# V's projection jobs first, K's three rounds behind; V's weights loaded as f32 in four pieces and cast on the chip

## The chip, the cores and the metric

The kernel runs on the 8 cores of one Trainium2 chip. Each core computes one batch element of 2048 tokens by itself; no core waits for another. The time of a run is device microseconds of the slowest core.

## The reference, cut to what matters

One decoder layer. From one normalised input come the projections q, k, v, u and two gates; attention and a pooling branch are merged by the gates, and an MLP follows. The part that matters here is the first line and what becomes of k and v:

```python
h = rms_norm(x, norm_mix[l])
proj = h @ w_in[l]                                  # [B,S,IN_WIDTH]
q, k, v, u, g_a, g_p = jnp.split(proj, splits, axis=-1)
q = partial_rope(rms_norm(q.reshape(B, S, ATTN_HEADS, HEAD_DIM), q_norm[l]), pos)
k = partial_rope(rms_norm(k.reshape(B, S, ATTN_HEADS, HEAD_DIM), k_norm[l]), pos)
v = v.reshape(B, S, ATTN_HEADS, HEAD_DIM)
o_attn = moba_attention(q, k, v)                    # 256-token blocks, own block plus 3 chosen by q . mean(k)
o_pool = multiscale_pool(u, w_pool_grp[l], pool_scale[l])
merged = sigmoid(g_a) * (o_attn @ w_up_attn[l]) + sigmoid(g_p) * (o_pool @ w_up_pool[l])
x = x + merged @ w_out[l]
x = x + jnp.square(jax.nn.relu(rms_norm(x, norm_mlp[l]) @ w_ff1[l])) @ w_ff2[l]
```

x is f32, 2048 x 1024 a core; each of the weights of q, k, v and u is 1024 x 512 in f32, 2.1 MB.

## The kernel before, in words

The tokens are cut into 16 tiles of 128. A tile of x is loaded into one of four slots (`p0_load`, L382, on SP's queue), squared and summed on ScalarE (`p0_sq`, L388), multiplied by its reciprocal root and the gain on VectorE (`p0_mul`, L399), transposed on TensorE (`p0_tr`, L406, eight transposes) and copied to `hT` by VectorE or ScalarE (`p0_ev`, through `evict`, L372 and L377). Then come four jobs for each tile, one each for K, V, U and Q: eight matmuls of 128 x 512 into one of four PSUM banks (`proj_mm`, L429). A weight lies in `wqkvu[cg]` as bf16, loaded in two halves by GpSimd's queue (`load_w`, L338), which casts on the way; a job waits for the first half before its first four matmuls and for the second before the others.

A V job is only evacuated (`v_ev`). A K or Q job goes on: square on ScalarE (`qk_sq`, L435), reduction on VectorE (`qk_red`, L440), root on ScalarE (`qk_root`, L444), scaling on VectorE (`qk_scale`, L451 to L457), which frees the bank, rope on VectorE or GpSimd (`qk_rope`, L468 to L476), transposes on TensorE (`qk_tr`, L483; for K with sums over the tile, L489) and evacuation. A U job is evacuated and goes through band matmuls (L516, L520). When all of K is there, `make_kT2` copies kT in two halves (SP), and behind each half loads `c_ind` twice on GpSimd's queue, which waits for the copy. Attention's matmuls (L880) need both.

The order of all this is not written out. A planner at the start of the program takes tasks with a priority (the place of their job in the list `jobs`), an estimated duration and an earliest time, lays them on the engines in a list schedule, and the program is emitted in the order of the planned starts. On the chip each engine works through its own instructions in that order and waits in place for what is not ready; SP and GpSimd do the same with the loads that they issue. In `jobs` round r holds K of tile r, V of tile r-3, U of tile r-12 and Q of tile r-7:

```python
for cg, lag in ((CG_K, 0), (CG_V, 3), (CG_U, U_LAG), (CG_Q, 7)):
```

The first loads are written by hand in `first_loads`; later weights are tasks (`wq`, `wu`) that wait until a given x slot is written. When the planned attention begins, U jobs that are left are mixed into its steps. Behind this come gates, output projection and MLP.

## Time and profile before

| | before |
|---|---|
| three runs | 954.8, 955.9, 956.35 us, median 955.9 |
| the profiled run | 953.49 us, its span 952.4 us on core 7 (cores 947.3 to 952.4) |
| TensorE busy | 913.4 us, 96% of the span |
| VectorE, ScalarE, GpSimd busy | 461.5, 381.0, 75.3 us |
| 0 to 40 us | TensorE busy 18.6 us, DMA share 0.91 |
| 40 to 140 us | TensorE busy 92.6 of 100 us, VectorE 80.8 |

A row of a timeline names a start and a length in us, the engine, the line of the program, output and input, and how many instructions of the kind stand behind one another; in brackets stands how long the engine was idle before it and what ended that. Nearly all tiles are views of one buffer, so most names read `raw`, and lines tell the steps apart. "PE" is TensorE, "DVE" VectorE, "ACT" ScalarE, "POOL" GpSimd.

### The profile page before, as it was taken

The numbers are of one execution on the slowest core, as the hardware profiler recorded it, in microseconds if no ns is written. First come the engines' busy times: TensorE is split into PE (matmuls) and PEld (weight loads), VectorE is DVE, ScalarE is ACT, GpSimd is POOL, SyncE is SP. The second block draws the span as 40 slices with busy tenths as digits, with TensorE's granted clock in tenths as the row PEclk, the third lists the DMA queues.
The fourth block names the chain that finished last, engine by engine and source line by source line (L and its number), as shares of the span: only waits on it lengthen the run. The fifth ranks groups of instructions, "written<-read, shape, count | busy, mean of one in ns | idle before, by whom it ended". The sixth has DMA issues, their size and how long they took to land.

```text
span 952.4 us, 17253 instructions; the slowest of 8 cores (947.3 to 952.4 us)
## 1 busy us (share of the span) xinstructions
PE 913.4 (96%) x5772; PEld 469.2 (49%) x5772; DVE 461.5 (48%) x876; ACT 381.0 (40%) x738; POOL 75.3 (8%) x133
## 2 busy tenths in 40 slices
PE   3798999899999999999999999999999999999997
PEld 1344555667767764444444444444444444444443
DVE  2578877555532333434775444434444444444443
ACT  2566666798899982222004344031111221111120
POOL 4212110321000000100001000000000000000000
PEclk9899999999999999999999999999999999999999
DMA  8942023523433337793989904250064100001113
GB/s 196 212 121 68 2 73 89 85 44 76 65 65 63 68 59 130 155 216 79 194 131 154 140 1 57 36 86 1 1 89 59 31 1 1 1 0 77 60 64 155
DMA packets 57895, 76.31 MB, mean 80 GB/s; under 512 B 27792, under 2 KB 46224, under 8 KB 57552
## 3 DMA queue, kind: packets, MB, share of 16 engines
q0 software_dynamic: 24288, 40.28, 27.5%
q1 hardware_dynamic: 33520, 34.92, 13.5%
q8 instruction: 49, 0.80, 0.3%
q14 instruction: 38, 0.31, 0.1%
HBM read 98.41 MB, written 8.39 MB: 112 GB/s over the span
## 4 chain that ended last, share of the span: by engine, by line
PE 87%; DMA 6%; DVE 3%; issue 2%; ACT 1%; SPq 0%; POOL 0%; DVEq 0%; ACTq 0%; POOLq 0%
PE bank L1339 23%; PE bank L1313 23%; PE bank L986 10%; PE bank L429 8%; PE bank L880 6%; PE bank L1223 6%; PE bank L918 3%; PE bank L1000 3%; PE bank L1005 3%; DMA raw<-w_qkvu 3%; DMA raw<-x 2%; DMA raw<-w_slice 1%; PE bank L483 1%; DVE raw L399 0%; DVE raw L457 0%
## 5 line engine op out<-in xcount | busy, mean ns | idle before, releaser
L1320 ACT ACTIVATE raw<-bank 128x512 f32<-128x512 f32 x128 | 76.4, 597 | 375.8 <-PE bank L1313 317.2
L1313 PE MATMUL bank<-raw 128*128 128x512 bf16 x1024 | 223.1, 379 | 0.0
L1339 PE MATMUL bank<-raw 128*128 128x512 bf16 x1024 | 223.1, 379 | 0.0
L887 ACT ACTIVATE raw<-bank 128x512 bf16<-128x512 f32 x288 | 152.6, 613 | 19.3 <-PE bank L918 17.6
L1313 PEld LDWEIGHTS bank<-raw 128*128 128x128 bf16 x1024 | 100.4, 98 | 120.7
L1339 PEld LDWEIGHTS bank<-raw 128*128 128x128 bf16 x1024 | 100.0, 98 | 121.0
L1322 DVE SCALAR_TENSOR_TENSOR raw<-bank,raw 128x512 bf16<-128x512 f32 x128 | 88.5, 692 | 140.8 <-ACT raw L1320 140.7
L1345 DVE SCALAR_TENSOR_TENSOR raw<-bank,raw 128x512 f32<-128x512 f32 x128 | 96.1, 751 | 112.7 <-PE bank L1339 112.4
L429 PE MATMUL bank<-raw 128*128 128x512 bf16 x512 | 125.9, 395 | 13.5 <-DMA raw<-w_qkvu 7.6
L986 PE MATMUL bank<-raw 128*128 128x512 bf16 x512 | 122.5, 379 | 0.4 <-DMA raw<-w_slice 0.3
L880 PE MATMUL bank<-raw 128*128 128x256 bf16 x576 | 101.7, 272 | 1.8 <-ACT raw L887 1.2
L918 PEld LDWEIGHTS bank<-raw 128*128 128x128 bf16 x1088 | 70.9, 98 | 26.3 <-issue 1.1
L429 PEld LDWEIGHTS bank<-raw 128*128 128x128 bf16 x512 | 48.8, 100 | 70.0 <-issue 24.8
L918 PE MATMUL bank<-raw 128*128 128x65 bf16 x1088 | 79.8, 193 | 0.8 <-DVE raw L927 0.7
L1011 DVE SCALAR_TENSOR_TENSOR raw<-raw,bank 128x512 f32<-128x512 f32 x64 | 43.8, 686 | 73.5 <-PE bank L1005 56.0
L986 PEld LDWEIGHTS bank<-raw 128*128 128x128 bf16 x512 | 49.4, 98 | 49.6 <-issue 2.4
L991 ACT ACTIVATE raw<-bank 128x512 f32<-128x512 f32 x64 | 38.3, 598 | 73.3 <-PE bank L986 69.7
L1223 PE MATMUL bank<-raw 128*128 128x512 bf16 x256 | 55.4, 379 | 0.0
L1223 PEld LDWEIGHTS bank<-raw 128*128 128x128 bf16 x256 | 25.0, 98 | 30.2
L880 PEld LDWEIGHTS bank<-raw 128*128 128x128 bf16 x576 | 37.1, 97 | 4.8 <-issue 2.5
L140 POOL DMA_DIRECT2D raw<-w_ff x16 | 14.0, 880 | 283.6 <-PE bank L1313 86.1
L372 ACT ACTIVATE raw<-bank 128x512 bf16<-128x512 f32 (+1 forms) x39 | 25.9, 670 | 18.6 <-PE bank L429 14.7
(91 smaller groups left out, 604.1 us busy)
## 6 DMA issues: line engine op xcount, KB each, us to landing
raw<-x SPq DMA_DIRECT2D x32, 512.0 KB, 6.3
raw<-w_ff POOLq DMA_DIRECT2D x16, 1024.0 KB, 12.4
...
out<-raw SPq DMA_DIRECT2D x16, 512.0 KB, 2.6
raw<-w_qkvu POOLq DMA_DIRECT2D x8, 512.0 KB, 12.9
...
raw<-w_out POOLq DMA_DIRECT2D x4, 512.0 KB, 13.6
raw<-c_ind POOLq DMA_DIRECT2D x4, 256.0 KB, 6.2
```

What stands on the lines that cost most here:

```text
L429: t.group("pe", [lambda e, c=c: e.matmul(bank_f(bk), lhsT=hT[:, c, tt * 128:(tt + 1) * 128], rhs=wqkvu[cg][:, c, :], start=(c == 0), stop= ...
L880: fns.append(lambda e, kt=kt, j=j: e.matmul(bank_f(sb_)[:, j * 256:(j + 1) * 256], lhsT=ksel[:, pr, kt * 128:(kt + 1) * 128], rhs=qTz[:, h ...
L887: t.op("act", lambda e: e.activation(out=pt, in_=bank_f(sb_), func=AF.Exp, scale=0.125), reads=hb[sb_], writes=[b_PT[si % NPT]])
L918: fns.append(lambda e, dst=dst, c0_=c0_, kt=kt, ql=ql, last=last: e.matmul(dst, lhsT=pt[:, c0_:c0_ + 128], rhs=v_aug[:, kt, h, :], start=( ...
L986: t.group("pe", [lambda e, c=c: e.matmul(bank_f(bk), lhsT=w[:, c, :], rhs=hT[:, c, T0:T0 + 512], start=(c == 0), stop=(c == 7)) for c in c ...
L1011: t.op("dve", lambda e: e.scalar_tensor_tensor(out=dst, in0=dst, scalar=1.0, in1=bank_f(bk), op0=ALU.add, op1=ALU.mult), reads=hb[bk] + [b ...
L1223: t.group("pe", [lambda e, c=c, bk=bk, hf=hf: e.matmul(bank_f(bk), lhsT=mT[tt // 4][:, c, (tt % 4) * 128:(tt % 4 + 1) * 128], rhs=wout[:, ...
L1313: t.group("pe", [lambda e, c=c, j=j, bk=bk: e.matmul(bank_f(bk), lhsT=ffw1[s][:, c, j * 128:(j + 1) * 128], rhs=hT[:, c, tg * 512:(tg + 1) ...
L1320: t.op("act", lambda e, bk=bk, si_=si_: e.activation(out=sqz[si_], in_=bank_f(bk), func=AF.Square), reads=hb[bk], writes=[b_sqz[si_]])
L1322: t.op("dve", lambda e, bk=bk, si_=si_, j=j: e.scalar_tensor_tensor(out=a1T[ab][:, j, :], in0=bank_f(bk), scalar=0.0, in1=sqz[si_], op0=AL ...
L1339: t.group("pe", [lambda e, j=j, bk=bk, hf=hf, i=i: e.matmul(bank_f(bk), lhsT=a1T[ab][:, j, i * 128:(i + 1) * 128], rhs=ffw2[s][:, j, hf * ...
L1345: t.op("dve", lambda e, bk=bk, dst=dst, tt=tt: e.scalar_tensor_tensor(out=dst, in0=bank_f(bk), scalar=r2sq[:, tt:tt + 1], in1=dst, op0=ALU ...
```

## The change

In `jobs` V has lag 0 and K lag 3. V's weights are loaded by SP as f32 into `wv_st`, which lies where the Q and U weights will lie, in four pieces; x1 is asked for behind the second and x2 behind the third, x3 behind the fourth. Each piece is cast to bf16 by VectorE or ScalarE (`cast_wv`), a planned task; V jobs wait for the casts. K's weights go out on GpSimd's queue once x2 is written, Q's once x5 is, U's once the tile that is then last in slot 3 is (x11). A small activation at the start brings the ScalarE table load forward. The planner's times for loads and weights are new, an x load counts 2.2 us on SP, and the second kT copy no longer waits for the last V job.

```diff
+        wv_st = view(F0 + 16 * KB, [128, 8, 512], F32)
...
+        b_wvst = [Buf("wvst%d" % i) for i in range(4)]
+        b_wv = [Buf("wv%d" % i) for i in range(4)]
...
-            for cg, lag in ((CG_K, 0), (CG_V, 3), (CG_U, U_LAG), (CG_Q, 7)):
+            for cg, lag in ((CG_V, 0), (CG_K, 3), (CG_U, U_LAG), (CG_Q, 7)):
...
-                    reads=[b_hT[tt], b_wqkvu[cg][hf]], writes=hb[bk])
+                    reads=[b_hT[tt]] + (b_wv[2 * hf:2 * hf + 2] if cg == CG_V else [b_wqkvu[cg][hf]]),
+                    writes=hb[bk])
...
+            t.op("act", lambda e: e.activation(out=ss2[:, 0:1], in_=eps_c, func=AF.Square),
+                 reads=[b_eps], writes=[Buf("warm")])
             p0_load(0)
             t.dma("pool", ident_b, c_ident_d, writes=[b_ident])
             t.dma("sp", gmix_bc, gmix_vec_d, writes=[b_gmix_bc])
+            for i in (0, 1, 2, 3):
+                t.dma("sp", wv_st[:, 2 * i:2 * i + 2, :], w_qkvu_d[CG_V][:, 2 * i:2 * i + 2, :], writes=[b_wvst[i]])
+                if i in (1, 2):
+                    p0_load(i)
+            p0_load(3)
+            pool_setup()
+            t.wait_written("pool", b_xslot[2])
             load_w(CG_K)
-            pool_setup()
-            t.wait_written("sp", b_wqkvu[CG_K][0])
-            p0_load(1)
-            p0_load(2)
...
-            p0_load(3)
-            t.wait_written("pool", b_xslot[2])
-            load_w(CG_V)
+
+        def cast_wv(eng, i):
+            evict(eng, wqkvu[CG_V][:, 2 * i:2 * i + 2, :], wv_st[:, 2 * i:2 * i + 2, :], [b_wvst[i]], [b_wv[i]])
...
-        W_AT = {CG_K: 14.5, CG_V: 26.0, CG_Q: 37.0, CG_U: 48.0}
-        X_AT = [4.5, 15.0, 16.5, 20.0]
+        W_AT = {CG_V: 0.0, CG_K: 27.0, CG_Q: 40.0, CG_U: 51.0}
+        X_AT = [4.5, 10.2, 13.2, 16.2]
+        V_AT = [7.2, 8.7, 11.7, 14.7]
+        casts = [add("cast", -3.0 + i, [("dve", 0.7, lambda i=i: cast_wv("dve", i)),
+                                        ("act", 1.05, lambda i=i: cast_wv("act", i))], after=V_AT[i]) for i in range(4)]
...
-                x_ld[tt] = add("xld", pk - 9, [("sp", 0.45, lambda tt=tt: p0_load(tt))],
+                x_ld[tt] = add("xld", pk - 9, [("sp", 2.2, lambda tt=tt: p0_load(tt))],
...
-        add("wq", 4.0, [("pool", 2.0, lambda: load_w_after(CG_Q, 0))], deps=[muls[1]], after=26.0)
-        add("wu", 8.0, [("pool", 2.0, lambda: load_w_after(CG_U, 1))], deps=[muls[2]], after=34.0)
+        add("wq", 4.0, [("pool", 2.0, lambda: load_w_after(CG_Q, 1))], deps=[muls[2]] + casts, after=27.0)
+        add("wu", 8.0, [("pool", 2.0, lambda: load_w_after(CG_U, 3))], deps=[muls[4]], after=36.0)
...
-        add("kt2b", 0.0, [("sp", 0.5, lambda: make_kT2(1))], deps=[kt2_0, by_job[(CG_V, NT - 1)]])
+        add("kt2b", 0.0, [("sp", 0.5, lambda: make_kT2(1))], deps=[kt2_0])
```

How the instructions stand. TensorE at the start, before: a row of eight 128 x 128 matmuls is the transposing of an x tile (L406), eight of 128 x 512 are one job (L429), L483 and L489 are a K tile's transposes and sums.

```order
L406 MATMUL bank<-raw 128x128 x8
L429 MATMUL bank<-raw 128x512 x8
L406 MATMUL bank<-raw 128x128 x16
L429 MATMUL bank<-raw 128x512 x16
L406 MATMUL bank<-raw 128x128 x8
L429 MATMUL bank<-raw 128x512 x8
L483 MATMUL bank<-raw 128x128 x4
L489 MATMUL bank<-raw 128x2 x4
L429 MATMUL bank<-raw 128x512 x8
L406 MATMUL bank<-raw 128x128 x8
L483 MATMUL bank<-raw 128x128 x4
L489 MATMUL bank<-raw 128x2 x4
```

TensorE at the start, now; the same steps have the lines L409 and L432.

```order
L409 MATMUL bank<-raw 128x128 x16
L432 MATMUL bank<-raw 128x512 x8
L409 MATMUL bank<-raw 128x128 x8
L432 MATMUL bank<-raw 128x512 x8
L409 MATMUL bank<-raw 128x128 x8
L432 MATMUL bank<-raw 128x512 x16
L409 MATMUL bank<-raw 128x128 x8
L432 MATMUL bank<-raw 128x512 x16
L409 MATMUL bank<-raw 128x128 x8
L432 MATMUL bank<-raw 128x512 x8
L409 MATMUL bank<-raw 128x128 x8
L432 MATMUL bank<-raw 128x512 x16
```

Six tiles are transposed and five V jobs, then K0, stand ahead of the second K job; ten jobs, with eight tiles, stand ahead of the first K transpose, where before there were four jobs and four tiles.

ScalarE up to K's first statistics, before: a pair of L388 and L391 is the square of an x tile and its root, L435 the square of a K job, L444 the root for its scaling, L372 an evacuation.

```order
L388 ACTIVATE raw<-raw 128x1024
L391 ACTIVATE raw<-raw 128x1
L388 ACTIVATE raw<-raw 128x1024
L391 ACTIVATE raw<-raw 128x1
L388 ACTIVATE raw<-raw 128x1024
L391 ACTIVATE raw<-raw 128x1
L435 ACTIVATE raw<-bank 128x512
L372 ACTIVATE raw<-bank 128x8x128
L388 ACTIVATE raw<-raw 128x1024
L391 ACTIVATE raw<-raw 128x1
L444 ACTIVATE raw<-raw 128x8
L435 ACTIVATE raw<-bank 128x512
```

ScalarE at the same steps, now, from the square of x6 on: L391 and L394 are the x tile's pair, L439 the square of a K job, L448 its root, L375 an evacuation.

```order
L391 ACTIVATE raw<-raw 128x1024
L394 ACTIVATE raw<-raw 128x1
L391 ACTIVATE raw<-raw 128x1024
L394 ACTIVATE raw<-raw 128x1
L375 ACTIVATE raw<-bank 128x8x64
L391 ACTIVATE raw<-raw 128x1024
L394 ACTIVATE raw<-raw 128x1
L439 ACTIVATE raw<-bank 128x512
L391 ACTIVATE raw<-raw 128x1024
L394 ACTIVATE raw<-raw 128x1
L448 ACTIVATE raw<-raw 128x8
L439 ACTIVATE raw<-bank 128x512
```

Before, K0's square stands behind those of x0 to x2 and its root behind x3's; now its square stands behind those of x0 to x8 and its root behind x9's.

GpSimd ahead of attention, before: L468 to L476 are one rope, `c_ind` belongs to `make_kT2`.

```order
L468 TENSOR_TENSOR raw<-raw 128x128
L470 TENSOR_TENSOR raw<-raw 128x8x8
L473 TENSOR_TENSOR raw<-raw 128x8x8
L476 TENSOR_TENSOR raw<-raw 128x8x16
L140 DMA raw<-c_ind 32x2x2048 x4
L140 DMA raw<-w_up_pool 128x4x1024
```

GpSimd at the same place, now; L472 to L480 are one rope.

```order
L140 DMA raw<-c_ind 32x2x2048 x4
L472 TENSOR_TENSOR raw<-raw 128x128
L474 TENSOR_TENSOR raw<-raw 128x8x8
L477 TENSOR_TENSOR raw<-raw 128x8x8
L480 TENSOR_TENSOR raw<-raw 128x8x16
L140 DMA raw<-w_up_pool 128x4x1024
```

A rope, that of Q's tile 12, now stands behind the four loads.

## Rows read from the trace of the kernel before

**Rows 1.** Waits of TensorE, 0 to 160 us: total, times, longest.

```profile
PE bank L406 <- DVE raw L399: 14.1, 4, 9.6
PE bank L429 <- DMA raw<-w_qkvu: 7.6, 4, 4.2
```

**Rows 2.** Timeline of TensorE, 20 to 53 us: start, length, what.

```profile
22.76 5.63 PE L429 MATMUL bank<-raw 128*128 128x512 bf16 x16
...
28.23 0.61 PE L406 MATMUL bank<-raw 128*128 128x128 bf16 x8
...
35.06 1.86 PE L429 MATMUL bank<-raw 128*128 128x512 bf16 x4 [4.21 <-DMA raw<-w_qkvu]
...
41.35 5.34 PE L429 MATMUL bank<-raw 128*128 128x512 bf16 x24
...
51.08 1.89 PE L429 MATMUL bank<-raw 128*128 128x512 bf16 x8
```

**Rows 3.** Timeline of ScalarE, 0 to 50 us: table load, squares of x3, x4, x8.

```profile
4.74 1.28 ACT L388 ACT_TABLE_LOAD   x1 [4.74 <-DMA raw<-x]
...
24.28 1.06 ACT L388 ACTIVATE raw<-raw 128x1024 bf16<-128x1024 f32 x1 [2.49 <-DMA raw<-x]
...
27.34 1.06 ACT L388 ACTIVATE raw<-raw 128x1024 bf16<-128x1024 f32 x1 [0.27 <-DMA raw<-x]
...
45.93 1.06 ACT L388 ACTIVATE raw<-raw 128x1024 bf16<-128x1024 f32 x1 [0.27 <-DMA raw<-x]
```

**Rows 4.** Windows of 1 us: stretch, length, GpSimd busy, granted clock, DMA share, GB/s.

```profile
4.00:5.00 1.00, 1.00 (x2) 1.00 0.95 340
...
10.00:11.00 1.00, 1.00 (x1) 1.00 1.12 164
11.00:12.00 1.00, 0.48 (x1) 1.00 0.99 131
```

**Rows 5.** The page's part 6, DMA issues: count, KB each, us to landing.

```profile
raw<-w_qkvu POOLq DMA_DIRECT2D x8, 512.0 KB, 12.9
...
raw<-c_ind POOLq DMA_DIRECT2D x4, 256.0 KB, 6.2
```

**Rows 6.** Timeline of VectorE, 42 to 47 us, and one row of ScalarE, 20.77.

```profile
20.77 1.02 ACT L372 ACTIVATE raw<-bank 128x1024 bf16<-128x1024 bf16 x1
...
42.29 0.19 DVE L451 RECIPROCAL raw<-raw 128x8 f32<-128x8 f32 x1
...
43.40 0.67 DVE L440 TENSOR_REDUCE raw<-raw 128x8 f32<-128x512 f32 x1
...
44.84 0.29 DVE L476 TENSOR_TENSOR raw<-raw 128x128 bf16<-128x128 f32 x1
...
45.31 1.28 DVE L399 SCALAR_TENSOR_TENSOR raw<-raw 128x1024 bf16<-128x1024 f32 x1
```

**Rows 7.** Windows: PE, PEld, DVE, ACT, POOL busy, granted clock, DMA share, GB/s.

```profile
50.00:110.00 60.00, 52.61 (x355) 27.08 (x353) 49.13 (x124) 36.63 (x75) 9.88 (x20) 0.97 0.24 69
110.00:160.00 50.00, 50.00 (x350) 27.08 (x348) 38.74 (x112) 30.80 (x57) 5.39 (x13) 1.00 0.31 77
```

**Rows 8.** Timelines of GpSimd, SP and TensorE, 19 us and 126 to 165.

```profile
19.07 1.05 POOL L140 DMA_DIRECT2D raw<-w_qkvu  x2 [7.58 <-DMA raw<-x]
...
126.88 0.45 POOL L468 TENSOR_TENSOR raw<-raw 128x128 f32<-128x128 f32 x1 [0.64 <-DVE raw L453]
...
128.27 0.46 POOL L476 TENSOR_TENSOR raw<-raw 128x128 bf16<-128x128 f32 x1 [0.20 <-POOL raw L473]
...
133.58 0.24 PE L489 MATMUL bank<-raw 128*128 128x2 bf16 x4
...
136.10 0.54 SPq L140 DMA_DIRECT2D raw<-raw  x1
...
141.41 1.15 POOL L140 DMA_DIRECT2D raw<-c_ind  x2 [12.68 <-DMA raw<-raw]
...
164.27 0.38 PE L880 MATMUL bank<-raw 128*128 128x256 bf16 x2
```

More of the change, by code:

```diff
@@ L630, in first_loads @@
             t.dma("sp", rope_t, c_rope_d.rearrange("p (t n) -> p t n", t=NT), writes=[b_rope])
-            p0_load(3)
-            t.wait_written("pool", b_xslot[2])
-            load_w(CG_V)
+        def cast_wv(eng, i):
+            evict(eng, wqkvu[CG_V][:, 2 * i:2 * i + 2, :], wv_st[:, 2 * i:2 * i + 2, :], [b_wvst[i]], [b_wv[i]])
         first_loads()
         def load_w_after(cg, sl):
+            for b_ in b_wqkvu[cg]:
+                b_.fence = {b2.w[0]: 0 for b2 in b_wv}
+                for b2 in b_wv:
+                    b_.fence[b2.w[0]] = max(b_.fence[b2.w[0]], b2.w[1])
             t.wait_written("pool", b_xslot[sl])
             load_w(cg)
-        W_AT = {CG_K: 14.5, CG_V: 26.0, CG_Q: 37.0, CG_U: 48.0}
-        X_AT = [4.5, 15.0, 16.5, 20.0]
+        W_AT = {CG_V: 0.0, CG_K: 27.0, CG_Q: 40.0, CG_U: 51.0}
[3 more added lines that the diff above has]
+                                        ("act", 1.05, lambda i=i: cast_wv("act", i))], after=V_AT[i]) for i in range(4)]
         ji_of = {jb: ji for ji, jb in enumerate(jobs)}
@@ L648, in build_nc @@
         for tt in range(NT):
-            pk = ji_of[(CG_K, tt)]
+            pk = ji_of[(CG_V, tt)]
             if tt >= NXS:
-                x_ld[tt] = add("xld", pk - 9, [("sp", 0.45, lambda tt=tt: p0_load(tt))],
+                x_ld[tt] = add("xld", pk - 9, [("sp", 2.2, lambda tt=tt: p0_load(tt))],
                                deps=[muls[tt - NXS]] + ([prev_ld] if prev_ld else []))
@@ L657, in build_nc @@
             if x_ld[tt]:
-                sq_.after = -3.5
+                sq_.after = -2.0
             mul = Task("mul", pk - 3.5, [], deps=[sq_], get=["hb0"])
@@ L677, in build_nc @@
             nm = {CG_K: "pj_k", CG_Q: "pj_q", CG_V: "pj_v", CG_U: "pj_u"}[cg]
-            pj = Task(nm, ji, [], deps=[hev[tt]], get=["pj"], after=W_AT[cg])
+            pj = Task(nm, ji, [], deps=[hev[tt]] + (casts if cg == CG_V else []), get=["pj"], after=W_AT[cg])
             pj.opts = [("pe", 1.73, lambda ji=ji, k_=pj: proj_mm(ji, k_.slots["pj"]))]
@@ L749, in build_nc @@
         free_at = {n_: {i: 0.0 for i in v_} for n_, v_ in pools.items()}
-        eng_free = {"pe": 0.0, "act": 0.0, "dve": 0.0, "pool": 22.0, "sp": 20.0}
+        eng_free = {"pe": 0.0, "act": 0.0, "dve": 0.0, "pool": 20.0, "sp": 15.0}
         INF = 1e18
```

## The prediction

> **What bounds the kernel now.** I read the page first (TensorE busy nearly all the span, table above): time is TensorE's work plus what it loses, and an order can win only from the loss. The waits of TensorE over the first 160 us say where that is [rows 1]: 14.1 us in four waits for a multiply of x, 9.6 of them before the first tile is there at all, and 7.6 us in four waits for `w_qkvu`. The timeline of TensorE shows it in time [rows 2]. The row at 22.76 starts at half pace and ends at full pace (16 matmuls in 5.63 us where 16 at full pace take 3.46); V of tile 0 waits 4.2 us for the second half of V's weights, until 35.06, and comes back at half pace, 4 matmuls in 1.86 us. Full pace is read from the row at 41.35: 24 matmuls in 5.34 us less a tail of 0.16, 0.216 each, 1.73 us a job; the row at 28.23 gives 0.45 us for the eight transposes of an x tile in the same way. Up to 41.35 TensorE has done 5 jobs, 5 tiles of transposes and two K transposes with sums (0.3 each, the sums' row of 0.24 overlapping them): 11.5 us of work, 29.8 us lost. From there to attention's first matmul at 164.27 it loses about 10 us more, mostly between 50 and 110, where it is busy 52.6 of 60 us with VectorE at 49.1; from 110 to 160 it is busy all the time, with VectorE at 38.7 of 50 [rows 7]. Nothing that the diff touches lies behind that. So the stage to cost runs from 0 to 164.
>
> **The change, part by part.** *Loading.* V's weights now come as four f32 pieces of 0.52 MB on SP, behind x0 and the gain row, with x1 and x2 between. x0 landed at 4.74 [rows 3]. With only uncast traffic the engines moved 340 GB/s [rows 4], 1.54 us a piece, so x1 (fourth behind x0) lands at 10.9, x2 at 14.0, the last V piece (seventh) at 15.5, x3 at 17.1. With casting traffic the counter shows 131 to 164 GB/s [rows 4]; if that counts the written bf16, 262 to 328 of f32 are read, and by its low end a piece takes 2.0 us and the last V piece lands at 18.7. I take the uncast row, since nothing but a 32 KB constant is asked for on the other queue before x2 is in.
>
> *Casting.* Three casts on ScalarE at 1.02 us (its row of 1024 elements) and one on VectorE, at most 1.3 us (the multiply of 1024 f32 elements), at least 0.7 (the reduction of 512 elements) [rows 6]. The last one stands behind x2's square on ScalarE (14.0 plus 1.6), ends at 16.6, and holds V0's second half. VectorE's cast stands ahead of x1's multiply and delays it by about 1 us; hidden, since V0's second half waits for 16.6 anyway. With that cover gone it costs the 1 us.
>
> *First jobs.* V0 starts at about 16 at half pace and ends at 19.5; V1 I take as partly slow, as the row at 22.76 was [rows 2]. x3's chain (square, multiply, transposes, evacuation behind x4's square on ScalarE) gives V3 at about 26. K's weights are asked for at 14.2. A load of these took 12.9 us to land by the page's median [rows 5], V's whole pair 16.0 from its first issue at 19.07 to 35.06 [rows 2, 8]: so 27.5 to 30.5. K0 stands sixth among TensorE's jobs, which gets there at about 31: no wait, or little.
>
> *x against K and Q.* From 14 on, x tiles share the engines with the K and Q weights. Before, x3 was squared at 24.28, x4 at 27.34 and x8 at 45.93 [rows 3]: 3.1 us apart once, 4.65 on average after that. I take 3.2, because the longer gaps hold SP waiting for free slots, which the new order asks for earlier. x8 is then in at 35, x9 at 38.5, x11 at 45. The order listing shows what this holds up: ScalarE squares x8 before it squares K0, and x9 before K0's root. So K0's root comes at about 40; its scaling (1.2 us) and rope (1.1) on VectorE, with a reduction between [rows 6], end at 43.6. By 39.5 TensorE has done nine jobs (V0 to V5, K0 to K2) and eight tiles of transposes; all four job banks are then held, and it waits some 2 us for K0's. From there the K chains follow VectorE at about 3 us each (reduction, scaling, rope), and I get 14 jobs, 9 tiles and 3 K transposes by 52.9: 24.2 + 4.1 + 0.9 = 29.2 us of work. Before has 11 jobs, 6 tiles and 4 K transposes when the row at 51.08 ends at 52.97 [rows 2]: 22.9. **Term 1: 6.3 us won.** With pieces at 2.0 us it is 3.3; with K, x and Q all on time and no bank wait it is 9.
>
> *52 to 164.* Before lost about 7 us here to VectorE [rows 7]. Up to the round in which U joins, the new order asks VectorE for three K chains fewer (9 us of its work) and owes them after 110, where VectorE had 11 us free of 50. So part of the loss goes and part comes back: **term 2: 1.5 us won**, between 0 and 5.
>
> *kT2.* K's last tile is now three rounds later. Before, K15's sums ended at 133.8, the copy of kT was issued at 136.10, GpSimd's `c_ind` loads waited in place until 141.41, and attention began at 164.27 [rows 8]: 30.5 us of cover. In the new order nine jobs, three bands and four Q transposes stand there: 17.8 us. Both copies are now issued together, about 2.3 us behind the sums. One took 5.3 us until GpSimd went on; a second 1.05 MB behind it adds 3 at 340 GB/s [rows 4], so 8 or a little more. The last `c_ind` is issued 9 us behind the copies and lands 6.2 later [rows 5]: 17.6 behind the sums, and the step that needs it (head 4) stands at 20.9. Just covered. But the listing puts a Q rope (tile 12) on GpSimd behind the four `c_ind` issues, and GpSimd waits in place. It is free at 2.3 + 8 + 1.1 = 11.4 (1.1 for two issues, as at 141.41); the rope takes 1.85 (126.88 to 128.73), its transpose could start at 13.3, and TensorE reaches that transpose after three bands, five jobs and a transpose, 10.2 us. **Term 3: 3.1 us lost**, between 0 (TensorE later than back to back) and 6 (half pace for some us after it, as at 35.06).
>
> The early table load on ScalarE and the wait of U's weights for x11 (45; first U job near 90) cost nothing: V0 waits for its weights, not for x0, and U's weights, 16 us under way, have 29 us of cover.
>
> **Sum.** -6.3 - 1.5 + 3.1 = -4.7 us. Against the profiled run, 953.5 to 948.8; against the median of the runs shown, 955.9, to **951.2**.
>
> **What the Trainium skill says.** "DMA: Bandwidth & Descriptors", section Rules for kernel authors, wants loads of 1 MiB or more, and says that spreading DMAs over issuing engines saves only issue time, since all run on the same engines. By the fit in its section on the anatomy of a DMA (2.0 us fixed per load) seven pieces one after the other would take some 22 us, an estimate by that page, and V0 would start at 28; the row of 340 GB/s with two neighbouring 0.5 MB loads [rows 4] speaks against a fixed cost that isn't overlapped.
>
> **Rivals.**
> *Bigger win (0.20).* No loss in the tail and all of term 2: -6.3 - 5 = -11.3, 944.6. For it: VectorE had 11 us free late [rows 7]. Against: GpSimd's wait in place is in the trace [rows 8].
> *Slower (0.15).* x tiles come 4.65 apart, as x4 to x8 did [rows 3]. x8 is then in at 41, x9 at 46, x11 at 55; K0's root slips from 40 to 48 and TensorE, with four banks held, stands idle from 39.5 to 50 and returns at half pace, as at 35.06 [rows 2], 2.7 us. Term 1 becomes 6.3 - 8.2 - 2.7 = -4.6, the sum +6.2: 962. It decides against the change once x9 lands after about 44.
> *Same (0.15).* Leaving the cast out of the load saves nothing: the pieces come at the casting rate, 2.0 us. Term 1 is 3.3, the sum -1.7: 954.2. For it: the engines are as full, about 1.0, in the casting windows as in the uncast one [rows 4]. The Trainium skill's rule on issuing engines, just named, points the same way.
>
> **How the numbers follow.** My forecast, -2 to -8 us, has 0.50. A measurement can tell about 0.2%, 1.9 us, from no change. Faster takes nearly all of the forecast (0.48) and the bigger win: 0.68. Same: 0.17. Slower: 0.15. The range reaches from the bigger win to halfway into the slower case: 944.8 to 957.5.
>
> **What would show it.** V's first matmul near 16 and no wait of TensorE for `w_qkvu` over 2 us; K0's root at about 40, right behind x9's square; 13 to 15 jobs by 53; one wait of about 3 us of a Q transpose for GpSimd's rope, with GpSimd waiting for the second kT copy before it; attention's first matmul, with 62 jobs done instead of 60, near 163. If TensorE's idle time between 35 and 50 exceeds 5 us, or K's weights come after 34, term 1 is wrong; if TensorE waits more than 10 us between 52 and 110, term 2 is.

## The result, and the profile after

The changed kernel takes 962.71 us (median of 6 runs, 959.93 to 970.91) beside 955.35 us for the kernel before in the same session. The ratio is 1.0062, with an interval of 1.0037 to 1.0086: **slower by 0.6%**, where the prediction had 951.2 us and "faster" with a chance of 0.68. The time lies above the range, and close to the price of the rival *Slower*, 962. It will turn out that this rival's mechanism was there, that it was worth less than its price, and that most of the rest of the loss is a term which the prediction had and sized at a quarter. The profiled run took 961.18 us, with a span of 960.0 us on core 2 (cores 954.9 to 960.0). Every ratio leaves out the runs in which one die was slowed, such as the 970.91 us, and e7_pieces, slowed so in nearly all its runs, is read from the four cores of its other die.

**A ledger.** Two kernels that order the same work differently can't be compared by busy time, because a matmul at half pace is busy twice as long. So I count the weight loads of TensorE in a stretch, line by line, each at what its matmul takes at full pace (0.216 us for 128x512, as in the prediction, 0.057 for a 128x128 transpose or band, 0.109 for 128x256, 0.031 for 128x65), and call the rest of the stretch lost. The count is good to about 0.3 us a stretch. Times in us, slowest core of each profile (e11 below: core 5, 0.2 us under the slowest):

| | 0-53 | 53-100 | 100-150 | 150-190 | sum |
|---|---|---|---|---|---|
| before | 29.8 | 9.0 | 1.1 | 3.6 | 43.5 |
| after | 32.0 | 2.9 | -0.1 | 15.4 | 50.2 |
| difference | +2.2 | -6.1 | -1.2 | +11.8 | +6.7 |

The cores of one execution differ by more than the count does: up to 5.5 us in the first stretch of the changed kernel (26.5 to 32.0), 2 us in the others. The means of all eight cores tell the same story, 28.5, 9.2, 0.5 and 4.4 before, 30.3, 2.6, 0.3 and 15.2 after; but a difference of 1 or 2 us between two slowest cores decides nothing.

The sum nearly makes up the 7.6 us between the two spans. Up to 150 us the changed kernel is ahead by 5.1 us; it loses that and 6.7 more in 40 us, where K's last tile meets the start of attention.

The waits of TensorE in the changed kernel, 0 to 190 us (total, times, longest; the answer to [rows 1], whose waits ended at 160):

```profile
PE bank L409 <- DVE raw L402: 18.3, 4, 9.4
PE bank L432 <- ACT raw L375: 6.4, 2, 6.0
PE bank L487 <- POOL raw L480: 5.5, 1, 5.5
PE bank L520 <- DVE raw L380: 3.9, 3, 1.4
...
PE bank L432 <- DMA raw<-w_qkvu: 0.7, 1, 0.7
```

The waits for `w_qkvu` are gone, 0.7 us instead of 7.6. In their place stand three others: a wait of 6.0 us for an eviction by ScalarE, one of 5.5 us for a rope on GpSimd, and three for band evictions by VectorE.

**The first one, at 43 us.** Timeline of TensorE in the changed kernel (start, length; in brackets the idle time ahead of the row and what ended it), the answer to [rows 2]:

```profile
43.08 0.61 PE L409 MATMUL bank<-raw 128*128 128x128 bf16 x8
49.65 3.57 PE L432 MATMUL bank<-raw 128*128 128x512 bf16 x8 [5.96 <-ACT raw L375]
```

and the timeline of ScalarE over the same time, the answer to [rows 3]:

```profile
42.11 1.06 ACT L391 ACTIVATE raw<-raw 128x1024 bf16<-128x1024 f32 x1 [2.64 <-DMA raw<-x]
...
43.55 0.58 ACT L439 ACTIVATE raw<-bank 128x512 f32<-128x512 f32 x1
46.81 1.06 ACT L391 ACTIVATE raw<-raw 128x1024 bf16<-128x1024 f32 x1 [2.68 <-DMA raw<-x]
...
48.25 0.29 ACT L448 ACTIVATE raw<-raw 128x8 f32<-128x8 f32 x1
48.44 0.57 ACT L439 ACTIVATE raw<-bank 128x512 f32<-128x512 f32 x1
48.92 0.58 ACT L375 ACTIVATE raw<-bank 128x512 bf16<-128x512 f32 x1
```

The rows at 42.11 and 46.81 are the squares of x8 and x9, and both times ScalarE had stood idle until the tile landed, 4.7 us apart. Behind the second one stand K0's root (48.25), the square of another K job and a V eviction (48.92): three small things, all held by a tile that nothing of them needs. TensorE has its four banks full, waits 6 us and returns at half pace: 8 matmuls in 3.57 us, where a row of 8 at full pace takes 1.89 [rows 2].

**The second one, at 155 us.** GpSimd in the changed kernel, the answer to [rows 8]:

```profile
152.05 1.14 POOL L140 DMA_DIRECT2D raw<-c_ind  x2 [17.75 <-DMA raw<-raw]
157.29 1.05 POOL L140 DMA_DIRECT2D raw<-c_ind  x2 [4.10 <-DMA raw<-raw]
158.36 0.47 POOL L472 TENSOR_TENSOR raw<-raw 128x128 f32<-128x128 f32 x1
...
159.76 0.45 POOL L480 TENSOR_TENSOR raw<-raw 128x128 bf16<-128x128 f32 x1 [0.20 <-POOL raw L477]
```

One row of VectorE:

```profile
159.66 0.29 DVE L457 TENSOR_TENSOR raw<-bank,raw 128x128 f32<-128x128 f32 x1 [4.28 <-POOL raw L477]
```

And TensorE, from K15's sums on:

```profile
144.39 0.24 PE L493 MATMUL bank<-raw 128*128 128x2 bf16 x4
...
160.36 0.58 PE L487 MATMUL bank<-raw 128*128 128x128 bf16 x4 [5.52 <-POOL raw L480]
161.17 3.17 PE L432 MATMUL bank<-raw 128*128 128x512 bf16 x7 [0.22 <-issue]
```

GpSimd waits in place for the first copy of kT, issues two loads, waits 4.10 us for the second copy, issues two more, and only then ropes Q's tile 12. VectorE's scaling of the next Q waits 4.28 us for the same rope, because the two share a buffer (`x16`). TensorE waits 5.52 us and comes back at half pace (7 matmuls in 3.17 us). Between 154.8 and 169.8 it loses 7.3 us by the ledger. Attention's first matmul stands at 169.81, 25.4 us behind K15's sums, and another 8.1 us are lost from there to the first gate product at 190.25, with the three waits for band evictions among them; the kernel before lost 2.9 us in that stage, from 164.27 to 182.66.

### The profile page after: what moved, and what is told of

The parts are those of the page before. It is cut to its first block, busy times and chain, and to the rows that moved or that the text cites. A ratio compares the mean times of both kernels' runs of the same rounds, so it can differ in the third digit from the quotient of the medians.

```text
span 960.0 us, 17189 instructions; the slowest of 8 cores (954.9 to 960.0 us)
## 1 busy us (share of the span) xinstructions
PE 907.8 (95%) x5668; PEld 470.1 (49%) x5772; DVE 459.8 (48%) x863; ACT 385.1 (40%) x744; POOL 78.7 (8%) x143
## 3 DMA queue, kind: packets, MB, share of 16 engines
q1 hardware_dynamic: 34096, 37.02, 13.8%
## 4 chain that ended last, share of the span: by engine, by line
PE 87%; DMA 6%; DVE 2%; issue 2%; ACT 2%; SPq 0%; POOL 0%; DVEq 0%; ACTq 0%; POOLq 0%
PE bank L1355 23%; PE bank L1329 23%; PE bank L1002 10%; PE bank L432 8%; PE bank L896 6%; PE bank L1239 6%; PE bank L934 3%; PE bank L1016 3%; PE bank L1021 3%; DMA raw<-x 3%; DMA raw<-w_qkvu 1%; DMA raw<-w_slice 1%; DMA raw<-raw 1%; PE bank L487 1%; ACT raw L903 1%
## 5 line engine op out<-in xcount | busy, mean ns | idle before, releaser
L1355 PE MATMUL bank<-raw 128*128 128x512 bf16 x1004 | 222.1, 379 | 1.1
L1329 PE MATMUL bank<-raw 128*128 128x512 bf16 x1003 | 221.9, 379 | 1.1
L903 ACT ACTIVATE raw<-bank 128x512 bf16<-128x512 f32 x288 | 153.3, 623 | 20.9 <-PE bank L934 17.7
L432 PE MATMUL bank<-raw 128*128 128x512 bf16 x495 | 121.2, 392 | 10.5 <-ACT raw L375 6.4
L1002 PE MATMUL bank<-raw 128*128 128x512 bf16 x477 | 116.4, 379 | 2.5 <-DMA raw<-w_slice 0.3
L432 PEld LDWEIGHTS bank<-raw 128*128 128x128 bf16 x512 | 48.8, 100 | 64.5 <-issue 17.5
L1239 PE MATMUL bank<-raw 128*128 128x512 bf16 x251 | 55.2, 379 | 0.3
L1016 PE MATMUL bank<-raw 128*128 128x512 bf16 x127 | 32.6, 379 | 0.1
```

The costliest lines, as they stand in the source:

```text
L432: t.group("pe", [lambda e, c=c: e.matmul(bank_f(bk), lhsT=hT[:, c, tt * 128:(tt + 1) * 128], rhs=wqkvu[cg][:, c, :], start=(c == 0), stop= ...
L903: t.op("act", lambda e: e.activation(out=pt, in_=bank_f(sb_), func=AF.Exp, scale=0.125), reads=hb[sb_], writes=[b_PT[si % NPT]])
L1002: t.group("pe", [lambda e, c=c: e.matmul(bank_f(bk), lhsT=w[:, c, :], rhs=hT[:, c, T0:T0 + 512], start=(c == 0), stop=(c == 7)) for c in c ...
L1016: t.group("pe", [lambda e, c=c: e.matmul(bank_f(bk), lhsT=w[:, c, :], rhs=o_attnT[:, c, T0:T0 + 512], start=(c == 0), stop=(c == 3)) for c ...
L1239: t.group("pe", [lambda e, c=c, bk=bk, hf=hf: e.matmul(bank_f(bk), lhsT=mT[tt // 4][:, c, (tt % 4) * 128:(tt % 4 + 1) * 128], rhs=wout[:, ...
L1329: t.group("pe", [lambda e, c=c, j=j, bk=bk: e.matmul(bank_f(bk), lhsT=ffw1[s][:, c, j * 128:(j + 1) * 128], rhs=hT[:, c, tg * 512:(tg + 1) ...
```

## The experiments

| | ratio to before | interval | lost 0-53 | 53-100 | 100-150 | 150-190 |
|---|---|---|---|---|---|---|
| after | 1.0062 | 1.0037-1.0086 | 32.0 | 2.9 | -0.1 | 15.4 |
| e1_tail | 0.9968 | 0.9954-0.9981 | 31.9 | 2.9 | -0.1 | 6.8 |
| e2_times | 0.9985 | 0.9973-0.9998 | 25.6 | 5.2 | 1.5 | 11.1 |
| e3_both | 0.9943 | 0.9923-0.9962 | 25.3 | 5.2 | 1.5 | 8.6 |
| e4_vfirst | 1.0155 | 1.0135-1.0174 | 30.3 | 12.0 | -0.1 | 12.5 |
| e5_kfirst | 1.0013 | 1.0003-1.0023 | 29.0 | 14.5 | 1.1 | 3.4 |
| e6_kuncast | 0.9980 | 0.9959-1.0000 | 28.0 | 10.6 | 1.1 | 4.1 |
| e7_pieces | none | | 30.5 | 2.0 | -0.1 | 17.7 |
| e8_bands | 0.9928 | 0.9904-0.9953 | 25.7 | 5.1 | 1.5 | 7.6 |
| e9_kearly | 0.9920 | 0.9899-0.9942 | 24.0 | 6.7 | 0.4 | 8.0 |
| e10_ropelate | 0.9946 | 0.9917-0.9975 | 26.0 | 6.9 | 0.1 | 7.4 |
| e11_uearly | 0.9964 | 0.9937-0.9991 | 30.1 | 2.2 | 0.1 | 7.6 |
| e12_ulate | 1.0022 | 0.9999-1.0046 | 29.7 | 9.3 | 1.3 | 3.3 |

A thousandth of the ratio is 0.95 us.

**e1_tail: the late ropes off GpSimd.**

```diff
-                        "dve", is_k, tt, k_.slots["x16"], k_.slots["qtok"]))]
+                        "dve", is_k, tt, k_.slots["x16"], k_.slots["qtok"]))][1 if ji >= 52 else 0:]
```

> The changed kernel, with the rotations of the last four Q jobs (numbers 52, 54, 56, 58) allowed on VectorE alone, so that none stands behind the c_ind copies on GpSimd. Theory: the 5.5 us for which TensorE waits at 160.4 for Q12's rotation, and the half pace behind it (7.3 us lost between 154.8 and 169.8), belong to that queue alone: the time falls by 5 to 8 us against the changed kernel, to 954.5 to 957.5, TensorE's waits between 150 and 170 sum to under 2 us, and attention's first matmul comes at 163 to 165. Rival: the start of attention hangs on the landing of kT2 and c_ind, which come as late as they do whatever the rotations do: the wait moves to another matmul, and under 2 us is won.

9.0 us faster than the changed kernel (0.9968 against 1.0062), more than the theory had, and under the kernel before. GpSimd still waits for both copies, and nobody waits for GpSimd:

```profile
152.24 1.15 POOL L140 DMA_DIRECT2D raw<-c_ind  x2 [17.93 <-DMA raw<-raw]
157.00 1.05 POOL L140 DMA_DIRECT2D raw<-c_ind  x2 [3.61 <-DMA raw<-raw]
162.03 0.76 POOL L140 DMA_DIRECT2D raw<-w_up_pool  x1 [3.98 <-PE bank L487]
```

TensorE starts attention here:

```profile
161.31 0.38 PE L896 MATMUL bank<-raw 128*128 128x256 bf16 x2
```

The copies and `c_ind` come at the same times as in the changed kernel, and attention starts 8.5 us earlier. The rival, that it hangs on their landing, falls. Up to 150 us the ledger is unchanged; from there the loss falls from 15.4 to 6.8 us, so with GpSimd's wait went the half pace, and part of what was lost behind attention's start too (4.9 us up to the first gate product at 180.15, where the changed kernel lost 8.1).

**e2_times: the planner told the times that the chip showed.** The loads are asked for in the same order; only the order of work on the engines follows.

```diff
-        W_AT = {CG_V: 0.0, CG_K: 27.0, CG_Q: 40.0, CG_U: 51.0}
-        X_AT = [4.5, 10.2, 13.2, 16.2]
-        V_AT = [7.2, 8.7, 11.7, 14.7]
+        W_AT = {CG_V: 0.0, CG_K: 35.0, CG_Q: 45.0, CG_U: 60.0}
+        X_AT = [5.5, 14.8, 17.4, 20.7]
+        V_AT = [10.1, 12.8, 16.5, 19.5]
...
-                x_ld[tt] = add("xld", pk - 9, [("sp", 2.2, lambda tt=tt: p0_load(tt))],
+                x_ld[tt] = add("xld", pk - 9, [("sp", 4.6, lambda tt=tt: p0_load(tt))],
```

> The changed kernel, with the planner told the arrival times that the chip showed (x tiles at 5.5, 14.8, 17.4, 20.7 and then 4.6 us apart, V's pieces at 10.1, 12.8, 16.5, 19.5, weights of K at 35, Q at 45, U at 60). Nothing else is edited; the loads are asked for in the same order. Theory: the 6 us for which TensorE stands at 43 to 50 come from ScalarE's queue alone, in which the squares of x8 and x9 stand ahead of V's evictions and K0's root: with the order made for the real times the gap is under 2 us, K0's root comes at 38 to 40, and 4 to 6 us are won (957 to 959). Rival: work is missing, not order; with x tiles 4.6 us apart and K's weights at 35 there is nothing for TensorE to do before them, the gap is spread over other waits, and under 2 us is won (961 to 963).

7.3 us faster than the changed kernel (0.9985 against 1.0062), more than the theory's 4 to 6. ScalarE's timeline in this kernel:

```profile
41.23 0.58 ACT L439 ACTIVATE raw<-bank 128x512 f32<-128x512 f32 x1
...
43.66 0.30 ACT L448 ACTIVATE raw<-raw 128x8 f32<-128x8 f32 x1 [0.16 <-DVE raw L444]
...
46.28 1.05 ACT L391 ACTIVATE raw<-raw 128x1024 bf16<-128x1024 f32 x1
...
49.90 1.06 ACT L391 ACTIVATE raw<-raw 128x1024 bf16<-128x1024 f32 x1
```

x8 and x9 are squared later than in the changed kernel (46.28 and 49.90 instead of 42.11 and 46.81). But K0's square and root stand ahead of both, the root at 43.66 instead of 48.25 (the theory had 38 to 40), and TensorE's wait of 6 us is gone. So the early loss was the order of the work, on ScalarE as its rows show, and not a want of work: 6.4 us less are lost by 53. But 3.9 of them come back between 53 and 150, and the larger part of what this kernel gains in the end, 4.3 us, lies behind 150, since the new order changes the tail as well.

**e3_both: the two edits together.**

> The two edits together: late Q rotations on VectorE alone, and the planner's arrival times as measured. Theory (two separate losses): the gains add, 9 to 14 us under the changed kernel, 949 to 953, which is under the kernel before. Rival (one loss, that work gained early stands waiting at K15's copies): the second edit gives nothing where the first is in, 954 to 958.

0.9943 is 11.4 us under the changed kernel, in the theory's range, though less than the sum of the two, 16.3. They are two losses, but the edits are not separate ones: in e2's order no rope stands right behind the `c_ind` loads any more. GpSimd is done with them at 151.11 and begins its next rope at 162.78; TensorE waited 2.0 us for ropes on GpSimd in all (5.5 in the changed kernel).

**e4_vfirst: the order alone.** The kernel before with V first, still with casting loads; the planner's times for the two weights change places, and the second kT copy waits for no V job, as in the changed kernel.

```diff
-            for cg, lag in ((CG_K, 0), (CG_V, 3), (CG_U, U_LAG), (CG_Q, 7)):
+            for cg, lag in ((CG_V, 0), (CG_K, 3), (CG_U, U_LAG), (CG_Q, 7)):
...
-            load_w(CG_K)
+            load_w(CG_V)
...
-            load_w(CG_V)
+            load_w(CG_K)
...
-            pk = ji_of[(CG_K, tt)]
+            pk = ji_of[(CG_V, tt)]
```

> The kernel before with the order of jobs alone changed: V leads, K three rounds behind, V's weights asked for first and K's second, both still by the casting loads on GpSimd in two halves as before; no pieces, no cast on chip, x tiles asked for as before, late rotations wherever the planner puts them. Theory (the order carries the gain in the middle and the loss at K15's copies, the loads carry the early part): early part as the kernel before, some 7 us won between 53 and 134, 10 to 13 lost at the tail: 957 to 963. Rival (the new loads cost the time): without them the order alone gives 948 to 953.

1.0155, slower than either theory had. The tail is as in the changed kernel (12.5 us lost, with a wait of 5.2 us for GpSimd's rope, below), so the order brings it. But the gain between 53 and 100 isn't there: 12.0 us are lost. TensorE's timeline shows the K weights at 35.5 and the rope wait:

```profile
35.52 1.86 PE L429 MATMUL bank<-raw 128*128 128x512 bf16 x4 [3.70 <-DMA raw<-w_qkvu]
...
167.37 0.59 PE L483 MATMUL bank<-raw 128*128 128x128 bf16 x4 [5.18 <-POOL raw L476]
```

and ScalarE's one tile that comes 13 us behind the tile ahead of it:

```profile
46.42 1.04 ACT L388 ACTIVATE raw<-raw 128x1024 bf16<-128x1024 f32 x1
...
59.20 1.06 ACT L388 ACTIVATE raw<-raw 128x1024 bf16<-128x1024 f32 x1 [6.45 <-DMA raw<-x]
```

With V leading, the new loads and the planner's times for them were worth 0.0155 less 0.0062, 8.9 us.

**e5_kfirst: the loads alone.** The changed kernel with K leading again, K's weights in the four pieces (`CG_V` and `CG_K` change places in the pieces, the casts, `load_w`, `W_AT` and `pk`).

```diff
-            for cg, lag in ((CG_V, 0), (CG_K, 3), (CG_U, U_LAG), (CG_Q, 7)):
+            for cg, lag in ((CG_K, 0), (CG_V, 3), (CG_U, U_LAG), (CG_Q, 7)):
...
-            load_w(CG_K)
+            load_w(CG_V)
```

> The new loads without the new order: K leads and V follows three rounds behind as in the kernel before, with K's weights loaded uncast in four pieces and cast on chip, x tiles between the pieces, and V's weights cast by GpSimd where the changed kernel loads K's. Theory (the two halves of the change add: with V leading, the new loads were worth 9 us, 0.0155 against 0.0062 above the kernel before): the loads alone give 944 to 949, and the tail has no wait on GpSimd at c_ind, as in the kernel before. Rival (they don't add: new loads only help where V's short chain leads, and the planner's too early times cost here what they cost the changed kernel): 952 to 960.

1.0013: with K leading the new loads are worth nothing to the slowest core, so the halves don't add. TensorE does start sooner, but then runs into two waits:

```profile
36.28 1.86 PE L432 MATMUL bank<-raw 128*128 128x512 bf16 x4 [5.52 <-DMA raw<-w_qkvu]
...
63.56 1.01 PE L409 MATMUL bank<-raw 128*128 128x128 bf16 x8 [6.60 <-DVE raw L402]
```

The first is V's second half, late as in the kernel before. The second is x9, squared at 59.15; five of the eight cores lose 13.7 to 14.6 us between 53 and 100, the other three 7.6 to 9.8. The tail is clean, 3.4 us, as the theory had: with K leading there is no rope behind the `c_ind` loads.

**e6_kuncast: K's weights uncast too.** From e3_both, K in four pieces on SP, cast on chip.

```diff
-            t.wait_written("pool", b_xslot[2])
-            load_w(CG_K)
...
+            t.dma("sp", wk_st[:, 2 * i:2 * i + 2, :], w_qkvu_d[CG_K][:, 2 * i:2 * i + 2, :], writes=[b_wkst[i]])
...
+            evict(eng, wqkvu[CG_K][:, 2 * i:2 * i + 2, :], wk_st[:, 2 * i:2 * i + 2, :], [b_wkst[i]], [b_wk[i]])
```

> The kernel of e3_both (late rotations on VectorE, times as measured), with K's weights too loaded uncast in four pieces on SyncE's queue, staged where kT comes later, and cast on chip by VectorE or ScalarE; x4 between the pieces; Q's and U's weights as before. Theory (a casting load moves its bytes more slowly than an uncast one, 209 to 245 GB/s in the slices with K's weights against 319 with V's pieces): x4 to x7 land 2 to 4 us earlier, K's first job comes at 32 to 34, and 2 to 4 us are won over e3_both (945 to 947). Rival (bytes are bytes, and all that lands early is bounded by one rate whatever its form, with the four casts as extra work on VectorE and ScalarE): e3_both's 949 within 1 us, or 1 to 3 us above it.

0.9980, 3.5 us above e3_both: the rival, and a little worse than it. Two things lie in this. The first is what a casting load costs. The DMA queues over the first 60 us (packets, MB, share of the 16 engines), of the kernel before:

```profile
q0 software_dynamic: 1440, 4.62, 50.1%
q1 hardware_dynamic: 2160, 6.60, 35.2%
```

of the changed kernel:

```profile
q1 hardware_dynamic: 2880, 9.22, 48.8%
q0 software_dynamic: 1025, 3.25, 35.0%
```

and of e6_kuncast:

```profile
q1 hardware_dynamic: 3456, 11.32, 60.1%
q0 software_dynamic: 864, 2.52, 27.7%
```

A share of 50.1% of 60 us is 30.1 us; so a counted MB of casting load (q0) takes 6.5, 6.5 and 6.6 us of all engines, and one of uncast load (q1) 3.2 in all three. But q0 counts the bf16 that is written. Over the whole program, the change takes 2.10 MB of f32 off q0, and its count falls by 1.05, while q1's rises by 2.10. Of the kernel before:

```profile
q0 software_dynamic: 24288, 40.28, 27.5%
q1 hardware_dynamic: 33520, 34.92, 13.5%
```

of the changed kernel:

```profile
q0 software_dynamic: 24000, 39.23, 26.4%
q1 hardware_dynamic: 34096, 37.02, 13.8%
```

So over these 60 us both forms cost 3.2 us a MB by f32 bytes read, some 310 GB/s, and leaving the cast out of the load saves no time on the engines. Over the whole program the two shares come to some 390 us before and 386 after, so that a saving of about 4 us of engine time elsewhere isn't ruled out. The Trainium skill, "DMA: Bandwidth & Descriptors", section Rules for kernel authors, says that loads issued by different engines run on the same 16 DMA engines, so that spreading them saves only issue time. The rows of the first 60 us agree: a MB that is read takes the same engine time from either queue.

The second is VectorE. Its cast of the first K piece waited for the piece, and x3's multiply stood behind it:

```profile
26.82 0.69 DVE L380 CAST raw<-raw 128x1024 bf16<-128x1024 f32 x1 [5.96 <-DMA raw<-w_qkvu]
...
28.68 1.28 DVE L402 SCALAR_TENSOR_TENSOR raw<-raw 128x1024 bf16<-128x1024 f32 x1
```

x3 had been squared at 19.97. It is the changed kernel's first wait over again, on the other engine.

**e7_pieces: the pieces first, x1 to x3 behind them.**

```diff
-                if i in (1, 2):
-                    p0_load(i)
-            p0_load(3)
+            for i in (1, 2, 3):
+                p0_load(i)
```

> The changed kernel with x1, x2 and x3 asked for after V's fourth piece instead of between the pieces; nothing else. Theory (one queue's transfers land in the order they are asked for, at one rate): V's fourth cast comes 3 us earlier (16 to 17), V0's job at 16 to 17, but x1 and x2 land at 18 to 20, so the second job waits for its tile as long as the first gained, and all that follows (x4 on) lands at the same time: within 1.5 us of the changed kernel's 961. Rival (the first jobs' start decides): 2 to 4 us faster, 957 to 959.

On those four cores the spans of the profiled run are 957.7 to 960.3 us; the changed kernel has 955.1 to 960.0 there. That is the theory's answer, though not by its details. V0 started at 22.13 and not at 17: x1's transposes stand ahead of it on TensorE, and x1, asked for last now, was squared at 17.99 and multiplied at 19.89. The row of the table is core 2's; on the mean of the four cores 31.0, 2.5, 0.1 and 15.9 us are lost in the four stretches, and 30.7, 2.7, 0.0 and 15.6 in the changed kernel. Where the x tiles stood among the pieces made no difference here.

**e8_bands: the late bands in other banks.** From e3_both.

```diff
-                bm.opts = [("pe", 0.47, lambda tt=tt, k_=bm, n_=tpn: band_mm(tt, k_.slots[n_]))]
-                tasks.append(bm)
+                bm.opts = [("pe", 0.47, lambda tt=tt, k_=bm, n_=bn: band_mm(tt, k_.slots[n_]))]
+                bm.only = gbank if ji >= NJ_Q else None; tasks.append(bm)
```

> The kernel of e3_both, with the band products of the last five U tiles written to banks 6 and 7 in turn with U's own products, instead of all to bank 3. Theory (the waits of 1.4 and 1.2 us for VectorE's eviction of bank 3 at 171 to 173, and the half pace of 3 us behind them, are that one bank): those waits go, and 2 to 3 us are won over e3_both (946 to 947). Rival (the fill for the first attention steps is short of work whatever bank it goes to, and the wait moves to an attention matmul): e3_both's 949 within 1 us.

0.9928 against 0.9943, with intervals that overlap. The band waits did shrink, from 2.6 us (e3_both, TensorE's waits)

```profile
PE bank L520 <- DVE raw L380: 2.6, 2, 1.4
```

to 0.8 (e8_bands):

```profile
PE bank L520 <- DVE raw L380: 0.8, 1, 0.8
```

but a wait of 2.3 us of an attention product for VectorE came in. The loss in the stretch falls by 1.0 us, which is within what cores differ by. Whether one bank for the bands costs anything stays open.

**e9_kearly: K early, with an order for it.** From e8_bands: K's pieces asked for right behind x3, the rope tables behind x5, Q's and U's weights behind x5 and x8, and the planner's times for that.

```diff
+        klds = [add("kld", (-5.0, -4.9, -3.9, -3.8)[i], [("sp", 1.65, lambda i=i: load_wk(i))], after=16.0) for i in range(4)]
...
+                x_ld[tt] = add("xld", pk - 9, [("sp", 1.65 if tt <= 5 else 3.2, lambda tt=tt: p0_load(tt))],
```

> The kernel of e8_bands, with K's weights uncast in four pieces as in e6_kuncast, but asked for right behind x3 (x4 between the pieces, x5 and then the rope tables behind them), Q's weights asked for once x5 has landed and U's once x8 has, and the planner told what 330 GB/s gives (pieces of K cast from 22, x tiles 1.65 us apart to x5 and 3.2 from there). Theory (all early loads read at one rate, so what counts is which bytes come first and whether the queues' order is written for the real times): K's last piece is cast by 31, K0's job comes at 30 to 33 instead of 37, TensorE is idle for under 3 us between 20 and 60, and 2 to 4 us are won over e8_bands (944 to 946). Rival (early work only goes to the head of another wait, at x tiles landing 3 us apart behind Q's and U's weights): within 1 us of e8_bands, or above it as e6_kuncast was.

0.9920, within e8_bands' interval, as the rival had it. The early part went as the theory said: K's jobs begin in a row that starts at 31.53, and TensorE idles 4.6 us between 20 and 60 (under 3 expected). It bought 1.7 us by 53 (1.0 on the mean of the cores) and gave back 1.6 (2.0) between 53 and 100, where TensorE waits for K and Q chains on VectorE:

```profile
79.30 5.29 PE L432 MATMUL bank<-raw 128*128 128x512 bf16 x16 [2.56 <-DVE raw L455]
```

This is the fastest version of the study, at 946.1 to 946.5 us beside 953.4 to 954.7 for the kernel before; of its 0.0080, 0.0057 are e1's and e2's together.

**e10_ropelate: the rope tables behind x5.** From e3_both.

```diff
+        gains, rld = {}, add("rld", -1.5, [("sp", 2.0, load_rope)], after=20.0)
```

> The kernel of e3_both, with the three small loads for the rotations (c_small, c_gv, c_rope) asked for behind x5 instead of ahead of x4; nothing else but the planner's due time for them (35). Theory (they hold the queue at 20 to 25 us, where the slices show 57 to 250 GB/s): x4 lands 1.5 to 2 us earlier than 27.9 and x5 than 32.0, and up to 1.5 us are won (947.5 to 949). Rival: x4 is held by K's weights on the other queue, so the tiles land where they did, and the time is e3_both's.

x4 and x5 were squared at 22.65 and 26.08 instead of 27.88 and 31.96, 5 to 6 us earlier and not 2. x6 and x7 then came at 37.02 and 42.04 instead of 35.27 and 39.62. The ratio is that of e3_both. What landed earlier here was paid for by what landed later.

**e11_uearly and e12_ulate: when U's weights are asked for.** The first from e1_tail, the second from the kernel before; the order of all other work is the same.

```diff
-        add("wu", 8.0, [("pool", 2.0, lambda: load_w_after(CG_U, 3))], deps=[muls[4]], after=36.0)
+        add("wu", 8.0, [("pool", 2.0, lambda: load_w_after(CG_U, 1))], deps=[muls[2]] + casts, after=29.0)
```

> The kernel of e1_tail with U's weights asked for right behind Q's, on the condition that x5 is in, as the kernel before asks for them behind Q's; every engine's order of work is the same. Question: where do the 7 us come from that the changed kernel wins between 53 and 100 us (2.9 lost there instead of 9.0). Theory (from the jobs: three K chains fewer on VectorE up to there): the loss in that stretch stays under 4 us, and the time within 1.5 us of e1_tail's 951.4. Rival (from the loads: U's weights go out 16 us later than before, so that x tiles land ahead of them): x10 and x11 land 4 us or more later, the loss in that stretch grows by 3 to 6 us, the time to 954 to 957.

> The kernel before, with U's weights asked for on the changed kernel's condition (once the tile is in that is then the last in the fourth x slot) instead of right behind Q's; nothing else. Theory (K's chains on VectorE hold the kernel before between 53 and 100): its 9.0 us of loss there stay within 1.5, and the time within 1.5 us of the kernel before. Rival (the bytes of U's weights hold its x tiles): 3 to 6 us are won, at 948 to 951.

e11 moved the load less than meant: the slot's last tile was x9 by then, so U's weights went out at 45.61 instead of 50.66. e12 moved it from 33.87 to 42.35:

```profile
42.35 1.12 POOL L140 DMA_DIRECT2D raw<-w_qkvu  x2 [7.84 <-DMA raw<-x]
```

The loss between 53 and 100 stayed at 2.2 (2.9 in e1_tail) and 9.3 (9.0 before), and neither became faster by more than its interval (e12 came out 2.1 us slower, with an interval from 0.1 faster to 4.4 slower). So the gain in the middle isn't the hour of U's load, as far as 5 to 8 us of shift can tell.

## Why the prediction was wrong, step by step

| | predicted | measured |
|---|---|---|
| Term 1, 0-53 | 6.3 won | 2.2 lost |
| Term 2, 53-150 | 1.5 won | 7.3 won |
| Term 3, behind K15 | 3.1 lost | 11.8 lost |

**Loading.** V's pieces were taken at 1.54 us each, the last one in at 15.5 and x3 at 17.1. The last cast started at 19.54 behind its piece, and x3 was squared at 20.74. From x0's square at 5.54 on, eight loads of 0.52 MB had landed in 15.2 us, 276 GB/s, not 340. The rate came from one window of 1 us [rows 4]; windows of 5 us in the changed kernel give

```profile
5.00:10.00 5.00, 0.60 (x7) 0.63 (x8) 1.45 (x2) 1.44 (x3) 4.76 (x3) 1.00 1.02 244
10.00:15.00 5.00, 0.41 (x4) 0.15 (x2) 0.69 (x1) 2.30 (x3) 0.41 (x1) 1.00 1.00 319
15.00:20.00 5.00, 1.60 (x10) 1.13 (x11) 2.54 (x4) 3.16 (x7) 1.07 (x2) 1.00 0.80 245
```

(the last number is GB/s). V0 started at 19.20 instead of 16:

```profile
18.40 1.01 PE L409 MATMUL bank<-raw 128*128 128x128 bf16 x8 [7.98 <-DVE raw L402]
19.20 3.62 PE L432 MATMUL bank<-raw 128*128 128x512 bf16 x8
```

It was held by x1's transposes, which stand ahead of it and wait for x1's multiply, and not by the last cast, as the prediction had it. The eight loads came 1.9 us apart, near the 2.0 of the rival *Same*, whose price of 3 us for a later V0 fits; its reason, that leaving out the cast saves nothing, is what e6's rows show.

The Trainium skill's fit of 2.0 us fixed per load ("DMA: Bandwidth & Descriptors", section on the anatomy of a DMA), which the page gives for loads that GpSimd issues, would have had V0 at 28, an estimate by that page for loads that wait for one another. Here SP issues them, and V0 stands at 19.20: loads in one queue did overlap (11 to 13 us from issue to landing, 1.9 from one landing to the next).

**x against K and Q: the step that failed in term 1.** The prediction chose 3.2 us between x tiles where its row gave 4.65 on average [rows 3], arguing that the long gaps were SP waiting for slots. (Its 3.2 from x3 at 17.1 gives x8 at 33.1, and not the 35 that it wrote; the slip is small beside the miss.) x8 and x9 landed 4.7 us apart. Both of its signs against term 1 came: TensorE waited some 7 us between 35 and 50, and the second half of K's weights held K0 until 35.30. All that the rival *Slower* says of place followed: x8 at 42 (41 named), x9 at 46.8 (46), K0's root at 48.25 (48), TensorE idle to 49.65 (50), half pace after it.

That rival priced term 1 at 4.6 lost, twice the 2.2 measured, and that price doesn't fit its own story: 6.3 won stand for 29.2 us of work by 53, so 4.6 lost leave 18.3, while nine jobs and eight tiles, which it had done by 39.5, are 19.2 already. With the 1.5 us that half pace allows from 50 to 53, its story gives 20.7, which is 2.2 lost, as measured. The trace has those nine jobs and eight tiles done at 43.7 and one job more by 53.

What the prediction had not seen is e2's point: the same tiles cost 6.4 us less by 53 when the queue is in another order. The prediction read the order, and saw what stands behind x8 and x9, and then asked only when the tiles come, not whether the order holds if they come late.

**52 to 164.** The sign was right and the size wrong: TensorE loses 2.8 us and not 10.1. VectorE is busy 52.4 us of the 60 from 50 on, 49.1 before, and TensorE 58.1 instead of 52.6 [rows 7]:

```profile
50.00:110.00 60.00, 58.09 (x384) 30.42 (x390) 52.40 (x140) 42.68 (x85) 11.73 (x26) 0.96 0.27 65
```

So VectorE was not spared work, as the prediction had it, but busier. Of the three K chains fewer, little is left by 100 us: nine K tiles and five Q tiles have then been through TensorE's transposes, before eleven and four, which is one chain fewer in all. e4 shows that V leading doesn't give this by itself, e5 that the loads don't. With both, e1, e7 and e11 lost 2.0 to 2.9 between 53 and 100, and those that had done more by 53 (e2, e3, e8, e9, e10) lost 5 to 7. So part of the term is work not yet due, and only the sum up to 150 should be read: 34.8 after, 39.9 before.

**kT2: the step that failed in term 3.** All its parts were in the prediction: the copies 2.3 us behind the sums (issued at 146.91, 2.3 behind 144.63), GpSimd free 11.4 behind them (at 158.34, 13.7 behind), the one rope on GpSimd. The 2.3 us by which GpSimd came free later and the 3.1 that were forecast make up the wait of 5.5. Three things were missing. The copies together took 10.4 us from issue to GpSimd's second pair, not 8. VectorE hangs on the same rope by `x16`, so nothing else gets ready meanwhile, and TensorE comes back at half pace; that makes 5.5 us of wait into 7.3. And the wait was taken to end there, while the stage behind it, in which only two projection jobs were left to fill attention's first steps (four before), lost 8.1 us instead of 2.9. That the fewer jobs are the reason is not shown. e1 took the wait away and 8.6 us went.

Terms 1 and 3 were off by 8.5 and 8.7 us, and term 2 by 5.8 the other way. That the time came out at the rival's 962 is therefore luck and no proof of its sum; what it had right is the place in the early part.

**What stays open.** Where the 6 us between 53 and 100 come from is not shown: neither half of the change gives them alone, nor does the hour of U's load. And even the best version loses 8.0 us between 150 and 190, the kernel before 3.6. e8 took the band waits away and 1.0 us went with them; the rest is waits of 0.3 to 2.3 us among VectorE, ScalarE and TensorE that no run here took apart.
